# Modulation vectors in four column groups of TensorE, and where their weights are computed

## Chip, core and metric

One NeuronCore of a Trainium2 chip runs the kernel. Its engines work side by side, each on a queue of its own: TensorE (PE; PEld is its weight load), VectorE (DVE), ScalarE (ACT), GpSimd (POOL) and SyncE (SP), which only issues DMAs here. The metric is the device time of one execution in microseconds.

## What is computed

Two layers (`DEPTH = 2`) over 512 latent tokens and 128 context tokens, width `D` = 1024. The part that matters here is the modulation:

```
mod = silu(cvec) @ w_ada + b_ada                  # cvec: c (latent) or c_ctx (context); w_ada is 1024 x 6144
sh1, sc1, g1, sh2, sc2, g2 = split(mod, 6)
u = rmsnorm(h) * (1 + sc1) + sh1                  # feeds q, k, v, the convolution branch and the gates
h = h + g1 * (merged @ w_out)                     # merged: attention and convolution, gated
u2 = rmsnorm(h) * (1 + sc2) + sh2
h = h + g2 * grouped_moe(u2)                      # 16 experts, two for each token
```

`mod` is a pair of rows (latent, context) of 6144 numbers a layer; `w_ada` is 24 MB a layer.

## The kernel before

Weights come in units of 1 MB (`UNIT` = 2048 floats in each of 128 partitions), numbered in the order of use: 8 of `w_ada` (`N_ADA1`), 6 for q, k and v, 4 for the convolution's input, 12 of `w_ada` (`N_ADA2`), 16 for gates and attention output, 4 for the convolution's output, 4 for `w_out`, 4 of `w_ada` (`N_ADA3`), then three for each expert. SyncE loads them in that order. There are two buffers in `raw`; the first `w_ada` units and the experts use two more, `raw_x`. A load waits until the buffer's last user is done (`raw_free`): for a `w_ada` unit that is TensorE, for the others it is the operation that makes `w_lo`. Those other units are split by ScalarE into `w_hi` and by GpSimd into `w_lo = raw - w_hi` (`lo`, L1860 and L1857), for three matmuls in place of one.

A `w_ada` unit goes to TensorE as it is, in fp32. The stationary operand is `cs`, two columns (silu of both vectors), and the weights stream, 512 columns at a time:

```
j, kh = divmod(u, 2)            # unit u: 512 columns of mod (block j), half kh of the 1024 rows
k = kh * 4 + c                  # four matmuls, c = 0..3, sum into the same two rows of one PSUM bank
ins = mm(ps[0:2, b, :], cs[:, :, k], raw_of(ada_unit(u))[:, c * 512:(c + 1) * 512], ...)
```

So two units give one block of 512 columns, and there are 12 blocks. VectorE adds the bias (`mrow`, L1223; `modulation(j)`), for which GpSimd has loaded `adab` (`bias(j)`, two DMAs), and GpSimd stores the block to DRAM (`mod_d`, L1789). At most two blocks are under way, since `mrow` and `adab` have two places.

The start of a layer needs blocks 0 to 3, shift and scale of `u`. When they are in DRAM, GpSimd reads them back as 32 rows of 128 (`mrt`), TensorE turns them (L428), and VectorE makes the columns `mcol`: a copy (L1231), plus 1 on the scale (L1233), times the norm's gain (L1236). ScalarE and VectorE then make `u_hi` and `u_lo` (L909, L1247, L1250), and TensorE starts on q, k and v (L453). GpSimd's queue has the first two `lo` behind the `mrt` loads.

Blocks 4 to 9 lie in the attention. There head h makes its values while the scores of head h + 1 are computed, in an order written out by hand. TensorE has one unit in each of heads 0 to 11, as four pieces of one matmul between `scores`, `p_transposes` and `values`. They all use PSUM bank 7, and a new block waits (`fill`) until VectorE has drained the block before; VectorE does this in heads 2, 4, ... 12. `q_transposes` (L496, L499) stand in odd heads.

Blocks 10 and 11 (half of g2 each) come behind `w_out`: two units ahead of the transposes of `u2`, two around the routing. VectorE drains them behind the routing, and GpSimd stores them ahead of the first gather of the experts.

Of the kernel before, what the change touches and what calls it, by code (L numbers as in the profile page):

```python
# [53 lines left out]
N_ADA1, N_QKV, N_GLU, N_ADA2, N_GATE, N_CO, N_OUT, N_ADA3 = 8, 6, 4, 12, 16, 4, 4, 4  # L54
# [6 lines left out]
U_ADA3 = U_OUT + N_OUT  # L61
U_MOE = U_ADA3 + N_ADA3
# [90 lines left out]
def _build(nc, io, out, ledger, ctx):  # L153
# [116 lines left out]
    gp = const("gp", [P, 2, DH])  # L270
# [17 lines left out]
    adab = at("adab", [2, 2, 512], F32, R_W + 24 * KB)  # L288
    mrow = at("mrow", [2, 2, 512], F32, R_W + 28 * KB)
# [34 lines left out]
    mrt = const("mrt", [32, P])  # L324
# [57 lines left out]
    def _(eng):  # L382
# [19 lines left out]
        with eng.Fori(0, DEPTH) as l:  # L402
# [162 lines left out]
            for h in range(NH):  # L565
# [15 lines left out]
                if modulating:  # L581
                    ada(u, (1,))
# [3 lines left out]
                if modulating:  # L586
                    ada(u, (2,))
# [7 lines left out]
                if modulating:  # L595
                    ada(u, (3,))
# [62 lines left out]

# [1384 lines left out]
```

## Time and profile before

| | us |
|---|---|
| median of 3 runs | 2268.37 |
| lowest, highest run | 2263.72, 2269.03 |
| span of the profiled execution, first to last instruction | 2264.1 |

| engine | busy us | share of the span |
|---|---|---|
| TensorE matmul | 1756.0 | 78% |
| TensorE weight load | 1386.0 | 61% |
| VectorE | 1387.5 | 61% |
| ScalarE | 845.7 | 37% |
| GpSimd | 547.7 | 24% |

The page reports the span of the profiled execution and no time of its own beside it; the runs are other executions. Busy shares are averages over stages with different limits: what an operation is worth is read from its stage, from what the engines there wait for. The mean granted clock of TensorE is 0.885 of full speed. Matmuls overlap in part, so the spacing of two starts says more than the mean duration of one (656 ns in the group of L414).

### The profile page before, as it was taken

To read this page: it belongs to the slowest core of one execution; us is meant where nothing else is said; L and a number is where in the kernel's file an instruction comes from. 1 tells how busy PE (TensorE), PEld (TensorE's weight loads), DVE (VectorE), ACT (ScalarE), POOL (GpSimd) and SP (SyncE) were. 2 spreads that over 40 slices of the span, in tenths; PEclk is the share of its full clock that TensorE was granted. 3 is DMA by queue.
4 is the path that set the end of the run, shared out by engine and by line. 5 is a ranking of instruction groups with operands and counts; after the bars stand their busy time and mean duration, and the time that the engine had idled before them with its cause. 6 is when DMAs were issued, how large, how long until landed. Compare 5 with 4: busy or idle time off the path is not lost.

```text
span 2264.1 us, 29330 instructions
## 1 busy us (share of the span) xinstructions
PE 1756.0 (78%) x8766; PEld 1386.0 (61%) x8766; DVE 1387.5 (61%) x2078; ACT 845.7 (37%) x1294; POOL 547.7 (24%) x388
## 2 busy tenths in 40 slices
PE   5799688888998873888749977888799878658880
PEld 0578454568998751666317874455699876436660
DVE  1458567789854343667462856768898254537754
ACT  2122455571223031657321234556412322147651
POOL 3332000014432223323132220000333222132231
PEclk9799799999999965999979987999899989569995
DMA  8222012112221633989941211211122244359975
GB/s 286 64 59 72 24 57 75 57 38 57 56 75 61 218 130 122 321 305 308 347 156 43 75 43 38 75 57 48 37 76 57 66 163 155 138 184 344 345 245 205
DMA packets 211573, 298.89 MB, mean 132 GB/s; under 512 B 12336, under 2 KB 147696, under 8 KB 211328
## 3 DMA queue, kind: packets, MB, share of 16 engines
q1 hardware_dynamic: 182976, 209.73, 28.6%
q0 software_dynamic: 17872, 46.28, 5.8%
q10 hardware_dynamic: 10560, 40.90, 4.8%
q8 instruction: 76, 1.25, 0.2%
q14 instruction: 89, 0.73, 0.1%
HBM read 267.20 MB, written 39.63 MB: 136 GB/s over the span
## 4 chain that ended last, share of the span: by engine, by line
PE 33%; issue 25%; DVE 18%; DMA 10%; POOL 6%; ACT 5%; DVEq 1%; ACTq 1%; POOLq 0%; SPq 0%
PE ps L467 6%; PE ps L453 5%; PE ps L650 5%; POOL w_lo L1860 5%; PE ps L414 4%; DMA raw<-in_w_down 4%; PE ps L531 2%; PE ps L726 2%; DVE probs L1400 2%; PE ps L511 2%; DVE gu_lo L1206 2%; PE ps L742 2%; PE ps L684 1%; PE ps L513 1%; DMA raw<-in_w_ada 1%
## 5 line engine op out<-in xcount | busy, mean ns | idle before, releaser
L1860 POOL TENSOR_TENSOR w_lo<-raw,w_hi 128x2048 fp32r<-128x2048 f32 (+1 forms) x68 | 298.3, 4393 | 614.9 <-ACT w_hi L887 614.9
L467 PE MATMUL ps<-u_hi,w_hi 128*128 128x320 f32 x768 | 245.9, 320 | 39.5 <-POOL w_lo L1860 29.8
L887 ACT ACTIVATE w_hi<-raw 128x2048 fp32r<-128x2048 f32 (+1 forms) x68 | 109.3, 1610 | 383.5 <-PE ps L453 152.9
L467 PE MATMUL ps<-u_lo,w_hi 128*128 128x320 f32 x768 | 243.5, 317 | 0.0
L467 PE MATMUL ps<-u_hi,w_lo 128*128 128x320 f32 x768 | 243.4, 317 | 0.0
L1510 DVE SCALAR_TENSOR_TENSOR cv<-glu,convw,cv 128x670 f32<-128x670 f32 x240 | 235.2, 1054 | 0.0
L414 PE MATMUL ps<-raw,cs 128*2 128x512 f32 x320 | 173.7, 656 | 30.5 <-DVE mrow L1223 22.3
L467 PEld LDWEIGHTS ps<-u_hi,w_hi 128*128 128x128 f32 x768 | 150.0, 195 | 43.3 <-issue 31.6
L1416 DVE TENSOR_TENSOR pt_lo<-ps,pt_hi 128x512 fp32r<-128x512 f32 x160 | 107.5, 688 | 84.1 <-ACT pt_hi L994 83.4
L994 ACT ACTIVATE pt_hi<-ps 128x512 fp32r<-128x512 f32 x160 | 92.4, 597 | 169.9 <-PE ps L531 168.8
L467 PEld LDWEIGHTS ps<-u_lo,w_hi 128*128 128x128 f32 x768 | 150.2, 196 | 0.1
L467 PEld LDWEIGHTS ps<-u_hi,w_lo 128*128 128x128 f32 x768 | 149.8, 195 | 0.0
L1383 DVE TENSOR_REDUCE nmax<-ps 128x1 f32<-128x640 f32 x128 | 104.3, 815 | 45.1 <-PE ps L513 44.9
L531 PEld LDWEIGHTS ps<-ident,probs 128*128 128x128 f32 x640 | 76.8, 151 | 83.6 <-issue 47.5
L531 PE MATMUL ps<-ident,probs 128*128 128x128 f32 x640 | 104.0, 297 | 24.3 <-DVE probs L1400 19.6
L1789 POOL DMA_DIRECT2D mod_d<-mrow x24 | 12.5, 520 | 451.1 <-DVE mrow L1223 450.2
L453 PE MATMUL ps<-w_hi,u_hi 128*128 128x512 f32 x240 | 97.8, 407 | 29.9 <-DVE u_lo L1250 17.7
L511 PE MATMUL ps<-k_hi,q_st 128*128 128x320 f32 x256 | 90.7, 361 | 38.3 <-DVE q_st L1368 32.5
L971 ACT ACTIVATE probs<-ps,nmax 128x640 f32<-128x640 f32 x128 | 101.3, 792 | 39.5 <-DVE nmax L1383 38.7
L726 PE MATMUL ps<-gu_hi,xt_hi 128*128 128x512 f32 x272 | 107.6, 396 | 5.0 <-DVE xt_lo L1722 5.0
L726 PE MATMUL ps<-gu_hi,xt_lo 128*128 128x512 f32 x272 | 107.1, 394 | 0.0
L726 PE MATMUL ps<-gu_lo,xt_hi 128*128 128x512 f32 x272 | 106.9, 393 | 0.0
(319 smaller groups left out, 4259.5 us busy)
## 6 DMA issues: line engine op xcount, KB each, us to landing
raw<-in_w_ada SPq DMA_DIRECT2D x40, 1024.0 KB
raw<-in_w_in SPq DMA_DIRECT2D x48, 512.0 KB
raw_x<-in_w_gate SPq DMA_DIRECT2D x32, 512.0 KB
raw_x<-in_w_up SPq DMA_DIRECT2D x32, 512.0 KB
raw<-in_w_down SPq DMA_DIRECT2D x16, 1024.0 KB
raw<-in_w_gate SPq DMA_DIRECT2D x32, 512.0 KB
raw<-in_w_up SPq DMA_DIRECT2D x32, 512.0 KB
raw_x<-in_w_down SPq DMA_DIRECT2D x16, 1024.0 KB
```

The costliest lines, as they stand in the source:

```text
L414: ins = mm(ps[0:2, b, :], cs[:, :, k], raw_of(ada_unit(u))[:, c * 512:(c + 1) * 512], start=(k == 0), stop=(k == 7))
L453: ins = mm(ps[:, bs[t], :], (u_hi, u_lo)[x][:, k, t * P:(t + 1) * P], (w_hi, w_lo)[w][:, s, c * 512:(c + 1) * 512], start=(k == 0 and w + ...
L467: ins = mm(ps[:, b, 0:HALF], (w_hi, w_lo)[w][:, s, cols(k):cols(k) + P], xs[x][:, k, half * HALF:(half + 1) * HALF], start=(k == 0 and w + ...
L511: mm(ps[:, b, 0:HALF], q_st[:, h % 2, t * P:(t + 1) * P], k_hi[:, g, i * HALF:(i + 1) * HALF], start=True, stop=False)
L531: ins = nc.tensor.transpose(ps[:, b, t * P:(t + 1) * P], probs[:, h % 2, t, kc * P:(kc + 1) * P], ident[:, :])
L650: ins = mm(ps[:, bs[t], :], (m_hi, m_lo)[x][:, k, t * P:(t + 1) * P], (w_hi, w_lo)[w][:, s, c * 512:(c + 1) * 512], start=(k == 0 and w + ...
L726: ins = mm(ps[:, 2, :], (xt_hi, xt_lo)[x][:, k, :], (gu_hi, gu_lo)[w][i][:, k, :], start=(k == 0 and w + x == 0), stop=(k == 7 and w == 1))
L887: act(w_hi[:, n % 2, 0:k], raw[:, n % 2, 0:k], ACT.Copy).then_inc(*A.up("a_hi", "w_hi", n))
L1383: v.tensor_reduce(nmax[:, h % 2, t:t + 1], ps[:, b0:b0 + 2, 0:HALF], axis=AX.XY, op=ALU.max, negate=True).then_inc(*V.up("v_max", "nmax", ...
L1416: v.tensor_tensor(pt_lo[:, k, :], ps[:, b, :], pt_hi[:, k, :].bitcast(F32), ALU.subtract).then_inc(*V.drained(("PT", h, kc)))
L1510: ins = v.scalar_tensor_tensor(out=cv[:, c, :], in0=src, scalar=convw[:, c, k:k + 1], in1=cv[:, c, :], op0=ALU.mult, op1=ALU.add)
L1860: g_.tensor_tensor(w_lo[:, n % 2, 0:k], raw[:, n % 2, 0:k], w_hi[:, n % 2, 0:k].bitcast(F32), ALU.subtract).then_inc(*G.up("g_lo", "w_lo", n))
```

## The change

A unit of `w_ada` is now one chunk of 128 rows by 2048 columns. Its four matmuls take 512 columns each and write four pairs of PSUM partitions, 0, 32, 64 and 96, which are four column groups of the array. Eight units give one block of 2048 columns, so there are 3 blocks: block 0 is shift and scale of `u` and comes at the start, blocks 1 and 2 come in heads 0 to 7, two units a head. None is left behind `w_out`. `mrow` and `adab` have one place, over 98 partitions, and the bias is added by four VectorE operations of 512 columns, one for each group. Block 0 does not go through DRAM: TensorE turns `mrow` itself, in four transposes of 128 x 128, and four VectorE copies pick the columns.

```diff
-N_ADA1, N_QKV, N_GLU, N_ADA2, N_GATE, N_CO, N_OUT, N_ADA3 = 8, 6, 4, 12, 16, 4, 4, 4
+N_ADA1, N_QKV, N_GLU, N_ADA2, N_GATE, N_CO, N_OUT = 8, 6, 4, 16, 16, 4, 4
@@ TensorE
-            def ada(u, rows, bank=None):
-
-                j, kh = divmod(u, 2)
-                b = fill(("ada", j), bank) if kh == 0 and rows[0] == 0 else fills.of["ada", j]
...
+            def ada(u, bank=None):
+
+                j, k = divmod(u, KC)
+                b = fill(("ada", j), bank) if k == 0 else fills.of["ada", j]
+                eng.wait_ge(*T.at("w_raw", ada_unit(u)))
+                for q in range(4):
+                    ins = mm(ps[32 * q:32 * q + 2, b, :], cs[:, :, k], raw_of(ada_unit(u))[:, q * 512:(q + 1) * 512], start=(k == 0), stop=(k == KC - 1))
...
-            eng.wait_ge(*T.at("mrt"))
-            eng.sem_inc(sems("passed_T"), 1)
-            ins = nc.tensor.transpose(ps[:, b, 0:32], mrt[:, :], ident[0:32, 0:32])
+            eng.wait_ge(*T.at("drained", ("ada", 0)))
+            for c in range(4):
+                ins = nc.tensor.transpose(ps[:, b, c * P:(c + 1) * P], mrow[:, c * P:(c + 1) * P], ident[:, :])
@@ TensorE, head h
-                    ada(u, (0,), 7)
+                    ada(N_ADA1 + 2 * h, 7)
                 scores(h + 1, 0)
...
                 scores(h + 1, 1)
-                if modulating:
-                    ada(u, (1,))
...
                 scores(h + 1, 2)
                 if modulating:
-                    ada(u, (2,))
+                    ada(N_ADA1 + 2 * h + 1, 7)
...
                 values(h, 4)
-                if modulating:
-                    ada(u, (3,))
@@ TensorE, behind w_out
-            for u in range(N_ADA1 + N_ADA2, N_ADA1 + N_ADA2 + 2):
-                ada(u, range(4), 7)
@@ SyncE
-                load(n, (r(n, 4), io["w_ada"][l, kh * 512:(kh + 1) * 512, j * 512:(j + 1) * 512].rearrange("(c p) n -> p c n", p=P)))
+                load(n, (raw_of(n), io["w_ada"][l, k * P:(k + 1) * P, j * UNIT:(j + 1) * UNIT]))
@@ VectorE
-                v.tensor_tensor(mrow[:, j % 2, :], ps[0:2, b, :], adab[:, j % 2, :], ALU.add).then_inc(*V.drained(("ada", j)))
+                for q in range(4):
+                    rows = slice(32 * q, 32 * q + 2)
+                    ins = v.tensor_tensor(mrow[rows, :], ps[rows, b, :], adab[rows, :], ALU.add)
...
-            v.tensor_copy(mcol[:, :, :, :].rearrange("p a b c -> p (a b c)"), ps[:, b, 0:32]).then_inc(*V.drained(("mcol",)))
+            for i in range(2):
+                for a in range(2):
+                    ins = v.tensor_copy(mcol[:, i, a, :].rearrange("p (y c) -> p y c", y=2), turned[:, a, :, :, i])
...
-                if h % 2 == 0 and 2 <= h <= 12:
-                    modulation(3 + h // 2)
+                if h in (4, 8):
+                    modulation(h // 4)
@@ GpSimd
-            for j in range(4):
-                modulation(j)
-                if j + 2 < 4:
-                    bias(j + 2)
...
-            for i in range(2):
-                dma(mrt[i * 16:(i + 1) * 16, :], mod_d[i, 0:2 * D].rearrange("(r p) -> r p", p=P), "mrt", *(("mrt",) if i else ()))
...
-            modulation(10)
-            modulation(11)
```

On TensorE's queue, the first part of a head before (`raw` is the modulation's first matmul of the head; rows with `k_hi`, `probs` and `v_hl` are scores, transposes and values):

```order
L414 MATMUL ps<-raw,cs 2x512
L508 REGISTER_ALU
L390 REGISTER_ALU
L511 MATMUL ps<-k_hi,q_st 128x320
L513 MATMUL ps<-k_lo,q_st 128x320
L511 MATMUL ps<-k_hi,q_st 128x320
L513 MATMUL ps<-k_lo,q_st 128x320
L531 MATMUL ps<-ident,probs 128x128 x4
L390 REGISTER_ALU
L540 MATMUL ps<-pt_hi,v_hl 128x512
L540 MATMUL ps<-pt_lo,v_hl 128x512
```

and the end of one of heads 0 to 7 of the change, around its second unit:

```order
L504 MATMUL ps<-k_hi,q_st 128x320
L506 MATMUL ps<-k_lo,q_st 128x320
L406 REGISTER_ALU
L408 MATMUL ps<-raw,cs 2x512 x4
L386 REGISTER_ALU
L524 MATMUL ps<-ident,probs 128x128 x4
L533 MATMUL ps<-pt_hi,v_hl 128x512
L533 MATMUL ps<-pt_lo,v_hl 128x512
```

A single matmul at four places of a head has become a row of four at two places.

On GpSimd's queue, the start of a layer before (`ISA` and `REGISTER_ALU` rows are waits):

```order
L1834 ISA
L1789 DMA mod_d<-mrow 2x512
L1834 ISA
L1789 DMA mod_d<-mrow 2x512
L1848 ISA
L1789 DMA mrt<-mod_d 16x128 x2
L1855 ISA
L1860 TENSOR_TENSOR w_lo<-raw,w_hi 128x2048
L1855 REGISTER_ALU
L1860 TENSOR_TENSOR w_lo<-raw,w_hi 128x2048
```

and of the change, at the same place:

```order
L1772 DMA adab<-in_b_ada 2x512
L1772 ISA
L1772 DMA n1col<-in_n_cols 128x8
L1827 ISA
L1830 ISA
L1835 TENSOR_TENSOR w_lo<-raw,w_hi 128x2048
L1830 REGISTER_ALU
L1835 TENSOR_TENSOR w_lo<-raw,w_hi 128x2048
```

The stores and the `mrt` loads are gone, and the first `w_lo` stands behind one wait, for the bias adds of block 0 (L1827), and that for its `w_hi` (L1830).

## Rows read from the trace of the kernel before

**Rows 1.** The page's costliest groups: the line of the modulation matmuls.
```profile
L414 PE MATMUL ps<-raw,cs 128*2 128x512 f32 x320 | 173.7, 656 | 30.5 <-DVE mrow L1223 22.3
```

**Rows 2.** The chain that ended last (start, length, what), both layers' starts.
```profile
31.21 17.34 PE ps L414 x40
...
54.92 1.74 DMA mrt<-mod_d
57.43 7.02 DVE mcol L1233
...
1114.51 22.02 DMA y_in<-y_d
...
1146.36 3.18 DMA adab<-in_b_ada
1152.12 3.66 DMA adab<-in_b_ada
...
1162.38 6.95 DVE mcol L1233
```

**Rows 3.** Timeline, first layer's start: start us, us, engine, line, operation, [idle before].
```profile
9.78 9.68 PE L414 MATMUL ps<-raw_x,cs 128*2 128x512 f32 x16 [9.78 <-POOL mrt L1815]
...
34.64 7.03 PE L414 MATMUL ps<-raw_x,cs 128*2 128x512 f32 x16
...
48.58 0.68 DVE L1223 TENSOR_TENSOR mrow<-ps,adab 2x512 f32<-2x512 f32 x1 [5.98 <-PE ps L414]
...
50.45 1.91 ACT L887 ACTIVATE w_hi<-raw 128x2048 fp32r<-128x2048 f32 x1 [25.21 <-DMA raw<-in_w_in]
...
55.42 8.97 POOL L1860 TENSOR_TENSOR w_lo<-raw,w_hi 128x2048 fp32r<-128x2048 f32 x2
...
57.21 0.19 DVE L1231 COPY mcol<-ps 128x32 f32<-128x32 f32 x1 [7.95 <-PE ps L428]
```

**Rows 4.** Busy time by stretch: length, PE, PEld, DVE, ACT, POOL, PEclk, DMA, GB/s.
```profile
31.20:41.00 9.80, 9.79 (x23) 1.96 (x24) 0.68 (x1) 0.00 (x0) 3.03 (x6) 1.00 1.03 383
41.00:48.60 7.60, 7.54 (x18) 1.36 (x16) 0.70 (x2) 0.00 (x0) 0.51 (x1) 1.00 0.30 88
```

**Rows 5.** The same view, second layer's start.
```profile
1130.00:1137.70 7.70, 3.13 (x8) 0.48 (x6) 4.82 (x4) 2.07 (x4) 1.07 (x2) 1.00 1.04 413
```

**Rows 6.** Timeline, second layer's start, POOL.
```profile
1160.30 8.98 POOL L1860 TENSOR_TENSOR w_lo<-raw,w_hi 128x2048 fp32r<-128x2048 f32 x2
```

**Rows 7.** Timeline behind the output projection of layer one.
```profile
811.13 10.82 POOL L1857 TENSOR_TENSOR gu_lo<-raw_x,gu_hi 128x2048 fp32r<-128x2048 f32 x2 [7.13 <-ACT gu_hi L891]
812.07 5.54 DVE L1565 SCALAR_TENSOR_TENSOR u<-h_a,rstd,a_row 128x1024 f32<-128x1024 f32 x1
```

**Rows 8.** Busy time by stretch: heads 1 to 7, heads 8 to 11, single heads.
```profile
276.25:387.22 110.97, 94.21 (x436) 56.08 (x435) 80.35 (x167) 59.71 (x142) 4.53 (x9) 0.94 0.21 67
387.22:451.98 64.76, 54.67 (x249) 32.35 (x248) 45.56 (x95) 33.60 (x80) 2.01 (x4) 0.92 0.22 66
339.74:354.30 14.56, 12.92 (x67) 7.66 (x66) 11.96 (x26) 9.32 (x22) 0.00 (x0) 1.00 0.24 74
354.30:372.64 18.34, 14.93 (x61) 8.75 (x61) 10.86 (x23) 7.48 (x18) 1.49 (x3) 0.81 0.19 59
1559.72:1571.51 11.79, 9.57 (x55) 6.70 (x55) 10.85 (x23) 7.65 (x18) 0.51 (x1) 1.00 0.16 46
1571.51:1584.25 12.74, 9.15 (x58) 7.31 (x58) 12.07 (x26) 9.38 (x22) 0.00 (x0) 1.00 0.00 1
```

**Rows 9.** Timeline of PE in heads 5 and 6.
```profile
348.29 1.02 PE L414 MATMUL ps<-raw,cs 128*2 128x512 f32 x2
...
357.15 1.09 PE L531 MATMUL ps<-ident,probs 128*128 128x128 f32 x8 [0.68 <-DVE probs L1400]
...
360.64 1.87 PE L414 MATMUL ps<-raw,cs 128*2 128x512 f32 x2 [2.23 <-DVE mrow L1223]
```

**Rows 10.** Timeline ahead of the experts, POOL.
```profile
886.91 1.13 POOL L1789 DMA_DIRECT2D mod_d<-mrow  x2 [0.19 <-issue]
```

More of the change, by code:

```diff
@@ L1824, in bias @@
             def bias(j):
[L1826 to L1827 removed]
+                if j >= 1:
+                    eng.wait_ge(*G.at("drained", ("ada", j - 1)))
                     eng.sem_inc(sems("passed_G"), 1)
[L1829 to L1830 removed]
+                for q in range(4):
+                    dma(adab[32 * q:32 * q + 2, :], io["b_ada"][bass.ds(l, 1), j * UNIT + q * 512:j * UNIT + (q + 1) * 512].broadcast_to([2, 512]),
+                        "ada_b", *(("ada_bias", j) if q == 3 else ()))
             def modulation(j):
@@ L1835, in modulation @@
                 eng.sem_inc(sems("passed_G"), 1)
-                dma(mod_d[:, j * 512:(j + 1) * 512], mrow[:, j % 2, :], f"mod_st{j % 2}", "mod_out", j)
+                for q in range(4):
+                    dma(mod_d[:, j * UNIT + q * 512:j * UNIT + (q + 1) * 512], mrow[32 * q:32 * q + 2, :], "mod_st", *(("mod_out", j) if q == 3 else ()))
             bias(0)
-            bias(1)
             dma(n1col[:, :], io["n1_cols"][l], "g_n1", "n1_loaded")
-            for j in range(4):
-                modulation(j)
-                if j + 2 < 4:
-                    bias(j + 2)
-            eng.wait_ge(*G.at("mod_out", 2))
+            eng.wait_ge(*G.at("drained", ("ada", 0)))
             eng.sem_inc(sems("passed_G"), 1)
-            eng.wait_ge(*G.at("mod_out", 3))
-            eng.sem_inc(sems("passed_G"), 1)
-            for i in range(2):
-                dma(mrt[i * 16:(i + 1) * 16, :], mod_d[i, 0:2 * D].rearrange("(r p) -> r p", p=P), "mrt", *(("mrt",) if i else ()))
             def lo(n):
@@ L1889, in _ @@
             eng.sem_inc(sems("passed_G"), 1)
-            bias(4)
-            bias(5)
+            bias(1)
             eng.wait_ge(*G.at("k_done", LT))
@@ L1898, in _ @@
             g_.memset(ssq[:, 6:7], 0.0).then_inc(*G.up("g_c", "kv_free"))
-            for j in range(4, 10):
-                modulation(j)
-                if j + 2 < 10:
-                    bias(j + 2)
-            eng.wait_ge(*G.at("mod_out", 8))
-            eng.wait_ge(*G.at("mod_out", 9))
-            for n in range(U_GATE, U_ADA3):
+            modulation(1)
+            bias(2)
+            modulation(2)
+            eng.wait_ge(*G.at("mod_out", 2))
+            for n in range(U_GATE, U_MOE):
                 lo(n)
-            eng.wait_ge(*G.at(*used(U_ADA3 - 1)))
-            eng.sem_inc(sems("passed_G"), 1)
-            bias(10)
-            bias(11)
             for n in range(U_MOE, U_MOE + 2):
```

71 lines of the change are left out of this document (28 added, 43 removed).

## Prediction

> **What bounds the kernel now.** I read the chain that ended last first, to see which stages hold the end; then the timeline of each stage that the change touches; then the busy time by stretch for clock, DMA and the period of a head.
>
> Three places matter. First, the start of each layer. The reader is to see one line that is never parallel: TensorE computes units 3 to 7 back to back for 17.34 us, 40 records at 0.43 us each [rows 2]. VectorE then adds the bias (0.68 us), the row goes to DRAM and comes back by DMA, and TensorE turns it. VectorE's small `mcol` operation then takes 7.02 us (6.95 in the second layer) instead of a fraction of one, and it ends where GpSimd's two `w_lo` operations end (55.42 + 8.97 = 64.39; 57.43 + 7.02 = 64.45) [rows 2, 3]. The same pair ends at 1169.28 in the second layer and releases the same operation [rows 2, 6]. In the second layer the chain before it is not TensorE's but the bias DMAs: 3.18 us, then 3.66 us, one bank pair after the other [rows 2].
>
> Second, the attention heads. An odd head with its four modulation pieces takes 14.56 us with TensorE busy for 12.92 of it; a head without them takes 11.79 (even) or 12.74 us (odd), and VectorE is then the busiest (10.85 and 12.07) [rows 8]. So TensorE is the bound in heads 1 to 11 and VectorE in heads 12 to 15. Even heads take up to 18.34 us [rows 8]: TensorE stands 2.23 us until VectorE has drained bank 7, and comes out at the low clock (two records in 1.87 instead of 1.02 us) [rows 9].
>
> Third, ahead of the experts, two `mod_d` stores stand on GpSimd's queue before the first gather, 1.13 us [rows 10].
>
> **The price on which all hangs: a unit's four matmuls.** Before, one unit is four matmuls, each of which leaves two records in the trace (320 records for the 40 units in `raw` [rows 1]; 16 records, two units, in 7.03 us [rows 3]), so a unit takes 3.43 us at 2.4 GHz and twice that at 1.2. All write column group 0. After, the four write groups 0 to 3. No row here shows two matmuls in different groups. Bounds: nothing overlaps, 8 x 0.43 = 3.43 us; everything overlaps, two records deep, 0.86 us. Between them: a matmul's own two records go to the same group, so the second waits for the first, and if the queue also starts its instructions in program order, only the second record of one matmul lies beside the first of the next: 5 steps of 0.43 = 2.14 us for a unit alone. I take this value, because the 0.43 us spacing of all 40 records [rows 2] shows same-group records strictly behind each other; this is argued, not seen.
>
> The Trainium skill (TensorE: Matmul & The Clock Gate, Part 3: Packing small matmuls) gives 2.38x for three column tiles; carried on to four that would be an estimate of about 1.1 us for a unit, near the lower bound, and the sum would be some 2205 us. The same section says that a weight load overlaps a running matmul only where the row group differs; here all four share the rows, which would put a unit near the upper bound. No run here shows either.
>
> **Heads.** A piece (two records) holds TensorE for about 1.0 us [rows 9]; a lump of one unit would hold it 2.14 + 0.1 = 2.25. Each of heads 0 to 7 loses four pieces and gets two lumps, at the places of the first and third. First and third: +1.25 each. Second: -1.0. The fourth was free already, since TensorE waits 0.68 us for `probs` behind it [rows 9]. Sum +1.5; VectorE is near its own pace, so I take +1.3. Over heads 1 to 7 that is +9.1. Of their three stalls on bank 7 two go: the even head of the rows is 3.8 us longer than the odd one [rows 8], 3.5 taken, so -7.0. The one left (head 4) has four VectorE operations of 0.68 ahead instead of one: +2.0. So 110.97 becomes 115.1. Head 0: +1.3. Heads 8 to 11 lose everything: 64.76 us becomes twice 11.79 + 12.74 = 49.1, plus 2.7 for the modulation's four operations at head 8, which are now on the bounding engine: 51.8, a gain of 13.0 [rows 8]. Net 13.0 - 4.1 - 1.3 = 7.6 a layer, **15 us in both**. What is late next is VectorE. Its extra time at head 8 also holds the maxima queued behind it.
>
> **First layer's start.** TensorE stops being the bound and the loads take over: DMA is full until 41 us (share 1.03 at 383 GB/s) and nearly idle after it (0.30) [rows 4]. The eight units are the same 8 MB, so the last lands near 41 however fast TensorE is; its unit ends near 43 instead of 48.6. Then four bias adds (2.7), four transposes (8 take 1.09 [rows 9], so 0.5 to 0.8), four copies of at most 0.19 [rows 3]: `mcol`'s scalar operation is asked for near 47.3. Removed: a store, a load and the waits between (54.92 and before [rows 2]). But GpSimd's first `w_lo` now waits for the bias adds alone, and its `w_hi` began at 50.45 [rows 3], 5.3 us after TensorE released unit 6 (48.55 - 3.43 = 45.1), and took 1.91. With the release near 40.5 it ends near 47.3 to 47.7. The pair then holds VectorE until about 56.4 instead of 64.4: **8 us** (3 if TensorE stays the bound; 17 if `mcol` gets in first and what it meets afterwards is hidden). If it gets in first, `w_lo` meets the u pipeline instead, where one VectorE operation took 5.54 us beside GpSimd [rows 7], so most of the 9 us of the pair are paid again.
>
> The Trainium skill (SBUF — State Buffer, SBUF: two separate sides) says that the shared port is held for one whole instruction by whoever starts first. Row 57.43 shows VectorE waiting for both GpSimd instructions, so the measurement decides; by the rule alone VectorE would get in after the first, 4.5 us earlier a layer.
>
> **Second layer's start.** One group of four bias DMAs replaces the chain of pairs; its last lands where the second pair's did, 1149.5 [rows 2]. Bias adds to 1152.3, `w_lo` starts at 1152.6 instead of 1160.30: 7.7 us, and `mcol` waits for the pair again. Against it: DMA is saturated there (1.04, 413 GB/s [rows 5]) while `y_in` is on the chain for 22.02 us [rows 2]. Units 4 to 7 are now asked for earlier and in rows of 8 KB instead of 2 KB, so they take more of it. Up to 2.1 MB (two units) more ahead of `y_in` is 5 us; I take 2.5. **5 us.**
>
> **Ahead of the experts.** Two stores and their waits go, 1.3 us a layer: **2.6 us**. The four late units' matmuls cost nothing before: they lay beside VectorE's routing. The earlier loads of expert weights are hidden too.
>
> **Sum.** 15 + 8 + 5 + 2.6 = 30.6. The profiled execution's span is 2264.1, so 2233.5; the median of the runs is 4.3 above that span, so **2238 us**. A measurement of this kernel tells about 0.3%, 7 us, from no change.
>
> **Rivals.** *Full overlap* (0.86 us): lumps cost what a piece did, each head of 0 to 7 gets 1.0 shorter, heads give 52 us, the first start 11 (the last unit ends 1.3 us earlier, and in one case in four `mcol` gets in first): 70.6 in all, **2198 us**. For it: the groups share no output. Against: each matmul's two records. *No overlap* (3.43 us), the one on the other side: a lump is 3.54, each of eight heads grows by 2 x 2.54 - 1.0 = 4.1 (16 units where 12 were). Heads lose 29 us, the first start gives 3, the second 6, the experts 2.6: **2286 us**. Between 2.14 and 3.43 us a unit the sum goes from +30.6 to -17.4; it decides from about 2.96 us a unit, where the sum is nil. For it: every record in rows 1 to 3 is spaced as if alone. *The clock falls in heads 8 to 15*, where nothing fills TensorE any more: against it, heads without pieces ran at clock 1.00 with TensorE busy 9.57 of 11.79 us [rows 8]. If it did, a head grows by 0 to 7.4 us (twice 9.57 less 11.79), say 3.5, times 16: **2294 us**; it outweighs the gain from 1.9 us a head.
>
> **How the numbers follow.** Half overlap 0.47, full 0.20, none 0.20, clock 0.05, another mixture 0.08 (mostly faster). Faster 0.74, within 0.3% 0.06, slower 0.20. The range for eight in ten reaches from below full overlap, 2190, almost to none, 2285; half overlap alone gives 2224 to 2252, from the bounds of the first start and of the slip.
>
> **What would show it.** In the new trace: first to last start of a unit's eight records at 2.4 GHz: 1.7 to 2.1 us (half), under 1 (full), 3.4 (none). Heads 1, 3 near 15.9 us; heads 9, 10 near 12. `w_lo`'s first pair at about 47.5 and 1152.6 to 1155, with `mcol` ending beside it. `y_in` landing up to 3 us later than 1136.5. I am wrong if units overlap otherwise, if `w_lo` is later for want of `w_hi`, or if the lumps starve VectorE in heads 0 to 7.

## The result, and the profile after

| | us |
|---|---|
| before, median of 4 runs beside it | 2266.88 (2263.72 to 2269.03) |
| after, median of 4 runs | 2207.85 (2198.12 to 2209.05) |
| ratio, 95% interval | 0.9737 [0.9714, 0.9760] |
| span of the profiled execution after | 2196.6 |

The change is faster by 59 us, where the forecast had 30: the direction held, and the time lies inside the range, but at the place of a rival, full overlap (2198 us), not of the case that was called likeliest. The profiled execution (2198.12 us) is some 10 us below the other three, which have no trace; heads 8 to 12 below show one place that differs by 6 us from layer to layer.

The group that was most expensive for the modulation [rows 1], in the list of groups of the changed kernel (busy us, mean ns of one, idle before):

```profile
L408 PE MATMUL ps<-raw,cs 128*2 128x512 f32 x320 | 50.1, 706 | 22.4 <-DMA raw<-in_w_ada 17.3 <-DVE mrow L1201 5.0
```

The same 320 records keep TensorE busy for 50.1 us instead of 173.7, although one lasts a little longer. The next view, busy time in two short windows of one unit in head 1 at 2.4 GHz (length, PE, PEld, clock), shows why:

```profile
268.40:268.80 0.40, 0.36 (x4) 0.11 (x8) 1.00 0.00 0
268.40:269.50 1.10, 1.04 (x8) 0.11 (x8) 1.00 0.00 0
```

Four of the eight records run within the first 0.4 us, and all eight are done after 1.04 us: two rounds of four side by side, one round 0.43 us behind the other, and the last record is shown as 0.59 us long. The eight weight loads are all in the first window. The forecast took 2.14 us for this.

The chain that ended last, both layers' starts [rows 2]:

```profile
14.61 26.50 DMA adab<-in_b_ada
...
45.69 3.35 DVE mcol L1219
...
1073.22 28.49 DMA y_in<-y_d
...
1111.69 1.85 DMA adab<-in_b_ada
...
1118.13 3.10 DVE mcol L1219
```

TensorE is gone from the first start; what ends last is a DMA, the bias, which stands on GpSimd's queue behind the copies of `x_all` to `h_d`. The timeline of the first start [rows 3]:

```profile
38.92 1.89 PE L408 MATMUL ps<-raw,cs 128*2 128x512 f32 x8 [6.43 <-DMA raw<-in_w_ada]
41.13 2.84 DVE L1201 TENSOR_TENSOR mrow<-ps,adab 2x512 f32<-2x512 f32 x4 [4.76 <-DMA adab<-in_b_ada]
44.02 1.11 PE L421 MATMUL ps<-ident,mrow 128*128 128x128 f32 x4 [3.22 <-DVE mrow L1201]
44.47 8.98 POOL L1835 TENSOR_TENSOR w_lo<-raw,w_hi 128x2048 fp32r<-128x2048 f32 x2 [28.77 <-ACT w_hi L864]
45.69 3.34 DVE L1219 TENSOR_SCALAR mcol<-mcol 128x16 f32<-128x16 f32 x1
49.06 4.49 DVE L1222 TENSOR_TENSOR mcol<-mcol,n1col 128x8 f32<-128x8 f32 x2
```

TensorE stands 6.43 us for the last unit and is done 1.9 us after it starts. VectorE's first `mcol` operation ends with GpSimd's first `w_lo` (45.69 + 3.34 = 49.03; a `w_lo` takes half of 8.98), the next two with the second, at 53.5. "The pair" below means these two `w_lo`.

The heads, busy time by stretch [rows 8]: heads 1 to 7 and 8 to 11 of the first layer, then of the second:

```profile
263.54:361.88 98.34, 78.95 (x491) 53.23 (x491) 81.52 (x168) 60.25 (x142) 4.00 (x8) 0.95 0.45 151
361.88:413.61 51.73, 36.42 (x217) 29.42 (x216) 47.48 (x97) 34.18 (x80) 1.99 (x4) 0.97 0.03 7
...
1336.67:1435.88 99.21, 80.38 (x491) 54.62 (x491) 81.51 (x168) 60.30 (x142) 4.04 (x8) 0.93 0.45 149
1435.88:1490.95 55.07, 41.25 (x216) 35.01 (x216) 48.33 (x97) 34.10 (x80) 1.99 (x4) 0.85 0.02 7
```

110.97 us have become 98.34, and 64.76 have become 51.73 and 55.07. The account of both profiled executions, from the starts of the first or last record at each mark (q, k, v; the context's transpose in a head; the convolution's branch; the transposes of `xe`, the rows gathered for the experts):

| stretch | layer 1, before, after | layer 2, before, after |
|---|---|---|
| start of the layer to q, k, v (layer 2: from the last `xe`) | 83.6, 72.8 | 88.9, 85.6 |
| to head 0 | 192.6, 190.7 | 195.8, 191.7 |
| head 0 to head 12 | 187.5, 161.3 | 187.2, 167.4 |
| to the branch | 35.3, 36.8 | 37.5, 39.6 |
| to the first `xe` | 395.7, 394.6 | 394.7, 393.9 |
| experts | 204.8, 203.1 | 203.2, 203.0 |
| end, behind the last `xe` | | 57.2, 55.9 |

The stretches join, so the gains sum to the 67.5 us by which the spans differ: 46 in the heads, 14 in the starts, 2 ahead of the experts. The second row's 6 us were not forecast and lie, up to head 0, where the change touches nothing. In the first layer the convolution's input took 21.87 us at clock 1.00 after and 24.27 at 0.89 before. In the second, q, k, v and what follows them, before and after:

```profile
1188.50:1283.17 94.67, 88.57 (x361) 72.26 (x361) 40.42 (x45) 14.80 (x16) 25.07 (x8) 0.92 0.20 59
```
```profile
1144.93:1234.98 90.05, 83.95 (x361) 68.73 (x361) 38.97 (x41) 14.80 (x16) 25.44 (x8) 0.98 0.21 62
```

So these 6 us go, as far as they are traced, with a clock that came out otherwise in this execution, and the change itself is worth some 61 us of the 67.5; the medians say 59.

### The profile page after: what moved, and what is told of

Same layout as the page of the kernel before. It is cut to its first block, busy times and chain, and to the rows that moved or that the text cites. A ratio compares the mean times of both kernels' runs of the same rounds, so it can differ in the third digit from the quotient of the medians.

```text
span 2196.6 us, 29390 instructions
## 1 busy us (share of the span) xinstructions
PE 1626.6 (74%) x8772; PEld 1377.6 (63%) x8772; DVE 1393.7 (63%) x2084; ACT 847.4 (39%) x1294; POOL 530.5 (24%) x352
## 4 chain that ended last, share of the span: by engine, by line
PE 35%; issue 26%; DVE 17%; DMA 9%; POOL 6%; ACT 4%; DVEq 1%; ACTq 0%; POOLq 0%
PE ps L460 10%; PE ps L638 5%; PE ps L446 5%; POOL w_lo L1835 4%; DMA raw<-in_w_down 3%; PE ps L707 3%; PE ps L524 2%; PE ps L723 2%; DVE gu_lo L1182 2%; DMA y_in<-y_d 2%; PE ps L667 1%; DMA raw_x<-in_w_down 1%; PE ps L408 1%; DMA adab<-in_b_ada 1%; PE ps L504 1%
## 5 line engine op out<-in xcount | busy, mean ns | idle before, releaser
L524 PEld LDWEIGHTS ps<-ident,probs 128*128 128x128 f32 x640 | 84.0, 157 | 66.8 <-DVE probs L1386 33.4
L1705 DVE TENSOR_TENSOR xt_lo<-ps,xt_hi 128x1024 fp32r<-128x1024 f32 x36 | 44.1, 1225 | 104.0 <-ACT xt_hi L1117 104.0
L691 PE MATMUL ps<-ident,xe 128*128 128x128 f32 x288 | 42.2, 295 | 73.8 <-DMA xe<-u_d,gidx 73.8
```

The source lines that it names most:

```text
L524: ins = nc.tensor.transpose(ps[:, b, t * P:(t + 1) * P], probs[:, h % 2, t, kc * P:(kc + 1) * P], ident[:, :])
```

## The experiments

Each time stands beside its ratio to the kernel before on the same chip. Where an edit changes values, the router sends other numbers of rows to the experts, and that stage is then longer or shorter for a reason of its own: the count of `xe` transposes, from the lists of groups of the changed kernel and of rows_2k:

```profile
L691 PE MATMUL ps<-ident,xe 128*128 128x128 f32 x288 | 42.2, 295 | 73.8 <-DMA xe<-u_d,gidx 73.8
```
```profile
L691 PE MATMUL ps<-ident,xe 128*128 128x128 f32 x312 | 44.1, 288 | 75.1 <-DMA xe<-u_d,gidx 75.1
```

Of the first four runs I therefore compare stages, not times. Marks as in the account above; "start 2" is from the last `xe`; heads are 0 to 8 and 8 to 12, both layers. Each row is one execution. In spread and the kernels built on it (both_starts, adds_first, first_place), heads 8 to 12 also hold units and the second drain of bank 7, which the changed kernel has ahead of them:

| kernel | start 1 | start 2 | heads 0 to 8 | heads 8 to 12 |
|---|---|---|---|---|
| before | 83.6 | 88.9 | 128.1, 129.3 | 59.4, 57.9 |
| changed | 72.8 | 85.6 | 113.4, 113.3 | 47.9, 54.2 |
| one_group | 73.5 | 83.7 | 140.3, 144.2 | 48.1, 50.0 |
| two_abab | 72.8 | 84.0 | 121.8, 123.9 | 48.0, 48.0 |
| two_aabb | 72.9 | 84.6 | 124.4, 121.8 | 48.0, 51.5 |
| rows_2k | 75.4 | 84.2 | 113.2, 113.2 | 49.1, 54.2 |
| through_dram | 78.1 | 90.9 | 113.2, 113.1 | 54.2, 54.2 |
| lo_behind | 72.9 | 84.8 | 113.3, 114.4 | 49.1, 54.2 |
| stores_later | 68.3 | 80.2 | 113.2, 113.2 | 49.1, 49.1 |
| y_first | 73.2 | 80.3 | 113.1, 114.3 | 49.3, 52.8 |
| spread | 72.5 | 85.1 | 113.9, 112.6 | 57.3, 57.4 |
| both_starts | 67.9 | 76.7 | 112.7, 110.5 | 57.3, 57.3 |
| adds_first | 70.0 | 76.1 | 112.5, 112.6 | 57.3, 57.4 |
| filler | 72.8 | 84.7 | 113.2, 114.4 | 49.8, 49.9 |
| first_place | 67.9 | 73.5 | 106.4, 106.4 | 53.5, 53.5 |

### The unit's price: one_group, two_abab, two_aabb

```diff
                 for q in range(4):
-                    ins = mm(ps[32 * q:32 * q + 2, b, :], cs[:, :, k], ...
+                    g = q if k in (0, KC - 1) else 0        # two_abab: q % 2, two_aabb: q // 2
+                    ins = mm(ps[32 * g:32 * g + 2, b, :], cs[:, :, k], ...
```

> Units 1 to 6 of each block of eight put all four matmuls into column group 0 (units 0 and 7 stay as they are), so three quarters of the modulation is left out of the result; instructions, operands and waits are the same. Theory (the unit's price is the term that was mis-sized: the four groups run fully side by side): such a unit takes 8 x 0.43 = 3.43 us instead of 1.04 at 2.4 GHz, heads 1 to 7 grow by about 2 x 2.4 us each where both units are affected, 12 units a layer by 2.4 = 29 us, 57 in both layers, so about 2265 us. Rival (the gain came from fewer pieces and fewer stalls on bank 7, and the lump's length lies beside VectorE's work): less than half of that, 2220 to 2235 us.

> Units 1 to 6 of each block use two column groups in the order 0, 1, 0, 1 (half of the modulation is left out of the result). If every group is served by itself, each has two matmuls of two records, 4 x 0.43 = 1.72 us a unit instead of 1.04: +0.7 us for 24 units, about 2225 us. Strictly in program order it is the same 1.72, since neighbours always differ. If two groups only half overlap, as the prediction took for four: 8 records in 6 steps, 2.6 us, 2245 us.

> As two_abab, but in the order 0, 0, 1, 1 (half of the modulation is left out of the result). Theory that a matmul whose group is busy blocks those behind it, so that order counts: group 1 starts only when the last record of group 0 has started, 1.29 + 1.72 = 3.0 us a unit, +2.0 us for 24 units, about 2255 us. Rival that each group has a queue of its own and order doesn't matter: 1.72 us, as two_abab, about 2225 us.

Measured: 2244.87 us (ratio 0.9908 [0.9876, 0.9939]), 2198.62 (0.9708 [0.9674, 0.9742]) and 2217.52 (0.9805 [0.9767, 0.9842]), all with fewer rows in the experts (272, 272 and 280 transposes, where the changed kernel has 288; the experts of one_group take 196.6 and 193.4 us instead of 203, 16 of the 20 us by which 2265 was missed). One unit in a head of each, in the order above, by the timeline:

```profile
276.12 3.60 PE L409 MATMUL ps<-raw,cs 128*2 128x512 f32 x8
```
```profile
273.18 1.89 PE L409 MATMUL ps<-raw,cs 128*2 128x512 f32 x8
```
```profile
270.15 1.89 PE L409 MATMUL ps<-raw,cs 128*2 128x512 f32 x8
```

3.60, 1.89 and 1.89 us stand against 1.04 with four groups (seven, three, three and one steps of 0.43 us from the first start to the last, and 0.59 for the last record). Two_aabb is the one that tells most. The same windows as above show how many records run in its first 0.4 us, and in all, with one_group's first 0.4 us below:

```profile
270.10:270.50 0.40, 0.35 (x2) 0.10 (x4) 1.00 0.00 0
270.10:272.10 2.00, 1.89 (x8) 0.30 (x8) 1.00 0.00 0
```
```profile
276.10:276.50 0.40, 0.39 (x1) 0.09 (x2) 1.00 0.00 0
```

Two records run at once from the start in two_aabb, and in one_group only one. Records of one group start 0.43 us apart there, so the second record is group 1's, although in the program its first matmul stands behind all four records of group 0. So each group is served by itself, and a busy group doesn't hold the matmuls behind it: order within four matmuls cost nothing. The theory that a busy group blocks the others falls.

In the heads, one_group has 27 and 31 us more between heads 0 and 8, 2.4 to 2.8 for each of the 11 affected units there: the lumps lie on the path at their full price. The rival (their length is hidden beside VectorE) falls too. The two-group kernels have 8 to 11 us more.

### What the change does for the starts: through_dram, rows_2k, lo_behind

through_dram undoes one part, the turning of `mrow` by TensorE:

```diff
-            eng.wait_ge(*G.at("drained", ("ada", 0)))
+            modulation(0)
+            eng.wait_ge(*G.at("mod_out", 0))
             eng.sem_inc(sems("passed_G"), 1)
+            for i in range(2):
+                dma(mrt[i * 16:(i + 1) * 16, :], mod_d[i, 0:2 * D].rearrange("(r p) -> r p", p=P), "mrt", ...)
```

> The changed kernel with one part undone: block 0 goes from mrow to DRAM (four stores), comes back as 32 rows of 128 (mrt) and is turned by one transpose, and GpSimd's first two w_lo stand behind these DMAs, as before the change. Theory (the part is worth what GpSimd's pair is put back by): the bias adds end at 44.0, the store and its wait take about 5.6 us as before the change, so the pair starts near 49.6 instead of 44.5, mcol waits for it, and q, k, v start 5 us later in each layer: about 10 us more than the changed kernel, 2218 us. Rival (mcol gets in ahead of or between the pair, so that only the row's own way counts): 1 to 3 us a layer, 2210 to 2214 us.

2224.46 us, 0.9811 [0.9785, 0.9837]. Both starts are 5.3 us longer, as the theory said. In its timeline the pair begins at 49.91 and `mcol` ends with it:

```profile
48.87 1.03 POOL L1767 DMA_DIRECT2D mrt<-mod_d  x2 [2.19 <-DMA mod_d<-mrow]
49.91 9.00 POOL L1833 TENSOR_TENSOR w_lo<-raw,w_hi 128x2048 fp32r<-128x2048 f32 x2
51.68 0.19 DVE L1212 COPY mcol<-ps 128x32 f32<-128x32 f32 x1 [7.61 <-PE ps L422]
51.91 7.04 DVE L1214 TENSOR_SCALAR mcol<-mcol 128x16 f32<-128x16 f32 x1
```

The median is 16.6 us above the changed kernel's, the profiled span 26.2 us (2222.8 and 2196.6). Of the 26.2, 10.6 are these, 6.3 are heads 8 to 12 of the first layer (54.2 where the changed kernel's profile has 47.9), 3.9 the experts, and most of the rest lies ahead of head 0 and behind head 12: stages that the edit doesn't touch. What the 6 us in the medians beyond these 10.6 are isn't shown, as the other executions have no trace.

rows_2k loads the units as before the change:

```diff
-                load(n, (raw_of(n), io["w_ada"][l, k * P:(k + 1) * P, j * UNIT:(j + 1) * UNIT]))
+                load(n, (r(n, 4), io["w_ada"][l, kh * 512:(kh + 1) * 512, j * 512:(j + 1) * 512].rearrange("(c p) n -> p c n", p=P)))
```

> The w_ada units are loaded as before the change, 512 columns of 512 rows, in rows of 2 KB instead of 8 KB, and multiplied as if they were the others (same bytes, the modulation's values are wrong). Theory (8 KB rows take more of the DMA engines while y_in, in 4 KB rows, waits beside them): y_in takes some 22 to 24 us again instead of 28.5, and the time falls by up to 5 us, to about 2203 us. Rival (y_in is late because units 4 to 7 are asked for sooner, now that TensorE is through them faster, whatever their rows): 27 to 29 us, no change of the time beyond 2 us.

2237.68 us, 0.9886 [0.9848, 0.9923], with 24 transposes more in the experts, which took 211.9 and 224.8 us instead of 203; so the expected times can't be read from it. By stage: the last `y_in` tile comes 22.9 us after the last issue (1090.16 to 1113.03) where the changed kernel's chain has 28.49, so the size of the rows bears on how the DMA engines are shared. (In the kernels that load rows of 8 KB and leave the issue of loads and stores as it is, the last tile lands 26.2 to 28.5 us after its issue.) The last unit lands later for it in the first layer (TensorE is through it at 44.3 instead of 40.8). Start 1 is 2.6 us longer. Start 2, 84.2, lies among the 83.7 to 85.6 of the kernels with rows of 8 KB and a start otherwise unchanged: the rows of 8 KB cost nothing in sum.

lo_behind moves the pair behind `mcol`:

```diff
-            eng.wait_ge(*G.at("drained", ("ada", 0)))
+            eng.wait_ge(*G.at("acol"))
             eng.sem_inc(sems("passed_G"), 1)
             def lo(n):
```

> The changed kernel, but GpSimd waits for the finished mcol (acol) before its first two w_lo, not for the bias adds alone. Theory (paid again): mcol is done near 46.8 instead of 53.6 and u starts 6.8 us earlier, but the pair, now beside VectorE's u pipeline, costs about what it held VectorE for; in the run with rows of 2 KB one w_lo beside it lengthened the pipeline by 4.1 us, so two cost 8 us: between 2 us faster and 2 us slower a layer, 2204 to 2212 us. Rival (the pair fits into VectorE's waits for ScalarE in the pipeline): 5 to 6.8 us a layer less, about 2196 us.

2208.81 us, 0.9740 [0.9713, 0.9768], no change, and starts of 72.9 and 84.8. Without the pair beside it the last steps of `mcol` take 0.4 us instead of 7.9:

```profile
46.62 0.17 DVE L1219 TENSOR_SCALAR mcol<-mcol 128x16 f32<-128x16 f32 x1
46.82 0.24 DVE L1222 TENSOR_TENSOR mcol<-mcol,n1col 128x8 f32<-128x8 f32 x2
```

`u_hi` starts at 49.06 instead of 53.67, and `u_lo` is nevertheless done at 72.35, where it was 72.21: the gain goes back into the `u` pipeline beside the pair. "Paid again" holds.

### Emptying the DMA queues at the starts: stores_later, y_first

```diff
-        for t in range(NT):
-            dma(h_d[t * P:(t + 1) * P, :], io["x_all"][t * P:(t + 1) * P, :], "h_st")
...
             dma(lnb[:, :], io["ln_b_cols"][l], "g_small", "small_loaded")
+            for t in range(NT):
+                eng.wait_ge(*G.at("h", t, previous=True))
+                eng.sem_inc(sems("passed_G"), 1)
+                dma(h_d[t * P:(t + 1) * P, :], h_cur[:, t, :], "h_st", "h_stored", t)
```

> The copy of x_all to h_d (2.6 MB from DRAM to DRAM, ahead of the first layer) and the stores of h_cur at the end of each layer become five stores of h_cur behind the first two w_lo of each layer. Theory (in the first layer the loads are the bound, and this copy shares the DMA engines with them until 41 us): the last w_ada unit lands near 32 to 34 us instead of 38.9, q, k, v start 5 us earlier in the first layer; in the second, the bias lands earlier, but VectorE comes to the adds only 1 us earlier, since xn ends at 1112.3 and the adds began at 1113.6: together 6 us less, about 2202 us. Rival (the copy takes a share that the loads couldn't use): no change of the first start beyond 1 us, 2207 us.

2197.41 us, 0.9694 [0.9661, 0.9728]. Start 1 falls by 4.5 us. TensorE is through the last unit at 35.4 (33.50 + 1.89), and the adds no longer wait for the bias; VectorE comes to them from `xn`:

```profile
33.50 1.89 PE L408 MATMUL ps<-raw,cs 128*2 128x512 f32 x8 [0.93 <-DMA raw<-in_w_ada]
36.39 2.83 DVE L1201 TENSOR_TENSOR mrow<-ps,adab 2x512 f32<-2x512 f32 x4
```

Start 2 fell by 5.4 us, of which I had expected 1: the stores shared the DMA engines with `y_in` too (from the last `xe` to the last tile 38.7 us instead of 42.4). That is 3.7 of the 5.4; the rest isn't traced.

```diff
+                    if n == 4:
+                        eng.wait_ge(*S.at("y_here", previous=True))    # VectorE raises it behind its wait for the fourth tile
                     eng.wait_ge(*S.at(*raw_free(n - 4)))
```

> The changed kernel, but SyncE issues units 4 to 7 of the second layer only when the fourth of the five y_in tiles has landed. Theory (y_in is late because these 4 MB share the DMA engines with it): y_in is landed 10 to 12 us after its first issue instead of 31, VectorE then sets the pace with 3.8 us a tile, h_cur is done near 1096 instead of 1105.5, and q, k, v start 8 to 9 us earlier in the second layer, about 2199 us. Rival (all bytes are needed anyway, and the w_in units for the first w_lo then come late by as much): no gain, 2205 to 2210 us.

2197.53 us, 0.9686 [0.9663, 0.9709]. VectorE now goes through `y_in` without a wait, and the last tile is taken up 31.5 us after the last `xe` instead of 42.4. 5.6 of these 10.9 us are lost again: units 4 to 7 were released only at 1094, and TensorE ends the last at 1113.65. Start 2 is 80.3, in between the two theories; `y_in` is landed 18.7 us after its first issue, not 10 to 12.

### The heads and the clock: spread, both_starts, adds_first, filler, first_place

```diff
-                modulating = 2 * h < N_ADA2
-                if modulating:
-                    ada(N_ADA1 + 2 * h, 7)
+                if h < 4:
+                    ada(N_ADA1 + 2 * h, 7)
...
-                if modulating:
-                    ada(N_ADA1 + 2 * h + 1, 7)
+                if h < 12:
+                    ada(N_ADA1 + 2 * h + 1 if h < 4 else N_ADA1 + 4 + h, 7)
```

Block 2 is drained in head 12 instead of head 8.

> The changed kernel, but the 16 units lie two in each of heads 0 to 3 and one, at the second place, in each of heads 4 to 11. Theory (a lone unit fits into TensorE's waits for VectorE): in the changed kernel a pair of heads with two units each takes 26.1 us and one without 24.0 at the high clock, so heads 4 to 11 would take 4 x 24.0 = 96 us, where four heads with two units and four without take 2 x 26.1 + 3.7 for the stall of head 4 + 48 = 104: 4 to 8 us less a layer. And if heads 8 to 13 lose the clock because TensorE is idle in them, they keep it: 7 us less in each layer that had lost it. Together about 2190 us. Rival (a unit costs its 0.5 us wherever it lies): nothing from the first part, and 2200 to 2208 us, depending on the clock alone.

2214.17 us, 0.9776 [0.9748, 0.9805]: no gain, and both theories miss it, since an odd head with one unit takes longer (15.04 us) than one with two (13.74). Its clock by stretch, heads 9 and 10 of the second layer, and what TensorE did in the first of them:

```profile
1463.79:1478.83 15.04, 11.57 (x66) 8.93 (x66) 12.14 (x26) 9.22 (x22) 0.00 (x0) 0.89 0.20 70
1478.83:1491.08 12.25, 9.60 (x61) 6.75 (x61) 10.19 (x22) 7.54 (x18) 0.00 (x0) 1.00 0.22 85
```
```profile
1465.71 0.66 PE L489 MATMUL ps<-ident,q_tok 128*128 128x128 f32 x4 [0.69 <-ACT ctxp L960]
1467.33 0.33 PE L492 MATMUL ps<-ident,q_tok 128*128 128x128 f32 x1 [0.96 <-DVE cpt_lo L1407]
1467.52 1.06 PE L524 MATMUL ps<-ident,probs 128*128 128x128 f32 x8
1468.34 0.31 PE L550 MATMUL ps<-cpt_hi,v_hl 128*128 128x128 f32 x1
1468.48 0.27 PE L550 MATMUL ps<-cpt_lo,v_hl 128*128 128x128 f32 x1
1470.07 0.63 PE L504 MATMUL ps<-k_hi,q_st 128*128 128x320 f32 x1 [1.32 <-DVE q_st L1353]
1470.50 0.47 PE L506 MATMUL ps<-k_lo,q_st 128*128 128x320 f32 x1
```

TensorE idles 0.69, 0.96 and 1.32 us, with matmuls between, and what follows the last runs at 1.2 GHz (0.47 us for the second `scores` matmul, which takes 0.31 at the high level). In the changed kernel a unit lies in that last gap in heads 0 to 7, and nothing does in heads 8 to 15. Filler puts matmuls there that nobody reads:

```diff
+                if 9 <= h < NH - 1:
+                    if h == 9:
+                        eng.wait_ge(*T.at("drained", ("ada", 2)))
+                    for q in range(4):
+                        mm(ps[32 * q:32 * q + 2, 7, :], cs[:, :, 0], mrow[:, :], start=True, stop=True)
```

> The changed kernel, with four more matmuls that nobody reads (four column groups, 512 columns, as a unit) at the first place of each of heads 9 to 14, the result is unchanged. Theory (the clock falls in heads 8 to 13 because TensorE idles there, 1.07 and 1.31 us ahead of q_transposes' last and of scores in an odd head, 1.50 us ahead of p_transposes in an even one, and in a layer where it has fallen it doesn't come back): with the gaps ahead of scores filled, heads 9 to 13 show 1.00, a pair takes 24.0 to 24.6 us in both layers, and the layer that took 54.2 us for heads 8 to 11 takes 48 to 50: about 2203 us. Rival (the gap ahead of p_transposes or of ctx scores decides, and the dummies only add work): 50 to 57 us in both, 2208 to 2218 us.

2196.57 us, 0.9694 [0.9673, 0.9714], where the changed kernel has 0.9737: the two intervals just touch, so more work cost nothing and may have gained. Heads 8 to 12 take 49.8 and 49.9 us. That alone settles nothing: changed, rows_2k, through_dram, lo_behind, stores_later and y_first have the same heads without filler, and their twelve layers take from 47.9 to 54.2 us, six of them under 49.8. Head by head it says more. Head 9 shows a clock of 0.88 or less in eleven of these twelve layers, and 1.00 in both of filler, as heads 11 and 13 do there. An even head still falls to 0.87 (10 in the first layer, 12 in the second). Heads 9 and 10 of the second layer, in the changed kernel and in filler:

```profile
1449.94:1463.83 13.89, 10.24 (x58) 8.65 (x58) 12.29 (x26) 9.32 (x22) 0.00 (x0) 0.88 0.01 1
1463.83:1476.89 13.06, 10.72 (x53) 9.49 (x53) 10.56 (x22) 7.71 (x18) 0.00 (x0) 0.74 0.00 1
```
```profile
1455.83:1468.58 12.75, 10.16 (x67) 7.43 (x66) 12.02 (x26) 9.41 (x22) 0.00 (x0) 1.00 0.00 1
1468.58:1479.94 11.36, 9.17 (x61) 6.97 (x61) 10.40 (x22) 7.69 (x18) 0.00 (x0) 1.00 0.00 1
```

Two kernels put the edits together, both_starts:

> Three edits together: h_d stored behind the first two w_lo (as in stores_later), units 4 to 7 of the second layer issued when the fourth y_in tile has landed (as in y_first, but released by ScalarE at its landing, not by VectorE behind its work), and the units spread over heads 0 to 11 (as in spread). If the effects add: first start 68.3 us instead of 72.8; in the second layer y_first gave the loads away for 5.6 us because VectorE released them late, so experts' end to q, k, v falls from 85.6 to 74 to 76 us; heads as in spread. About 2185 us. If the two edits on the second start share one effect (both only empty the DMA engines beside y_in), it stays at 80 us, 2190 us.

and adds_first:

> both_starts, and VectorE adds the bias of block 0 before it makes xn, not after. If the adds and the turning can lie beside the wait for std in the second layer, q, k, v start there up to 3 us earlier than in both_starts. Rival: GpSimd's pair starts earlier too and holds xn as it held mcol: no gain, or up to 5 us more.

2192.03 us, 0.9680 [0.9657, 0.9704] and 2196.37, 0.9698 [0.9673, 0.9722]. Start 2 of both_starts is 76.7, so the two edits add nearly (8.9 us, where they gave 5.4 and 5.3 alone); the heads are as slow as in spread. first_place below has the same edits there and shows 73.5, so this mark of one execution is good to some 3 us. In adds_first VectorE's five `xn` took from 37.77 to 49.67 us in the first layer, across the pair, instead of 3.4: the first start is 2.1 longer; the second is 0.6 shorter, which is within what one execution tells.

first_place is both_starts with the lone unit at the head's first place:

```diff
-                if h < 4:
-                    ada(N_ADA1 + 2 * h, 7)
+                if h < 4 or 4 < h < 12:
+                    ada(N_ADA1 + 2 * h if h < 4 else N_ADA1 + 4 + h, 7)
```

> both_starts, with the lone unit of heads 5 to 11 at the first place of the head (ahead of scores) in place of the second. In spread and both_starts an odd head with a lone unit took 15.04 us at clock 0.89, one with two 13.75 at 1.00. Theory (what counts is the gap ahead of scores, which a unit at the first place fills): odd heads 12.9 to 13.75, even ones 11.3 to 12.3, at 1.00, so a pair takes 24.2 to 26.1 us instead of 27.3, 4 to 11 us less a layer: 2170 to 2185 us. Rival (the place doesn't matter, a lone unit keeps TensorE busy too little): 15.0 and 12.3 again, 2192 us.

**2171.29 us, 0.9598 [0.9577, 0.9619]**, the fastest of all, 1.4% of the time before below the changed kernel's ratio. In heads 5 to 11 of each layer the lone unit now lies ahead of `scores` (head 4's stays at the second place). The next view is the busy time of heads 7 to 10 of the second layer:

```profile
1402.65:1415.38 12.73, 10.16 (x66) 7.40 (x66) 11.98 (x26) 9.44 (x22) 0.00 (x0) 1.00 0.25 83
1415.38:1426.76 11.38, 9.11 (x61) 6.90 (x61) 10.40 (x22) 7.70 (x18) 0.00 (x0) 1.00 0.28 94
1426.76:1439.56 12.80, 10.15 (x66) 7.43 (x66) 11.98 (x26) 9.44 (x22) 0.00 (x0) 1.00 0.24 84
1439.56:1452.55 12.99, 10.81 (x61) 7.72 (x61) 10.49 (x22) 7.81 (x18) 0.00 (x0) 0.87 0.29 81
```

Heads 7 to 9 run at 1.00, and with one unit each they take within 0.14 us what heads with none take at that clock (12.73 and 11.24 in the changed kernel's first layer); head 10 still falls to 0.87, and I have no cause for it. The kernel to compare with is both_starts, which differs in nothing but the place: heads 0 to 12 take 159.9 us in both layers instead of 170.0 and 167.8, 18 of the 20.7 us between the medians. The odd heads 5 to 11 are at 1.00 in both layers; in spread, both_starts and adds_first 23 of 24 such heads are at 0.89. The one that isn't, head 5 of both_starts' second layer, tells the clock from the rest:

```profile
1398.10:1411.85 13.75, 10.37 (x66) 7.46 (x66) 11.92 (x26) 9.32 (x22) 0.00 (x0) 1.00 0.23 78
```

At the second place a unit makes an odd head 1.0 us longer at the full clock (13.75 instead of 12.73), and the low clock adds 1.3 (15.04). In the even heads, at 1.00 in both kernels, the place alone is worth 0.9 us (12.25 and 11.38). The place decides, not the number.

## Why the prediction was right and wrong

**The unit's price is the step that failed.** It was put as "if the queue also starts its instructions in program order, only the second record of one matmul lies beside the first of the next: 5 steps of 0.43 = 2.14 us". A unit took 1.04 us at 2.4 GHz, which by the spacing of starts is two rounds of 0.43, the 0.86 us of the rival that the forecast gave a chance of 0.20. The first half of the argument holds (a group's own records are 0.43 us apart), the second doesn't: two_aabb shows that a group's matmuls start while those ahead of them wait. The reason given for the value, the even spacing of all records before, could not tell: all of them were in one group. The Trainium skill (TensorE: Matmul & The Clock Gate, Part 3: Packing small matmuls) was the better guide with its 2.38x for three column tiles: two groups gave 3.60 / 1.89 = 1.9, four 3.60 / 1.04 = 3.5. Its sentence that a weight load overlaps a running matmul only where the row group differs isn't borne out here, where all four share the rows: the eight weight loads lie within the first 0.4 us, beside four running records.

**Heads 1 to 7**: forecast 110.97 to 115.1 us, measured 98.34 and 99.21 (the latter from 112.14). The lump was put at 2.25 us, and 14 of them cost 1.2 each too much: 16.8 us, the whole difference in the first layer (one_group confirms the price, not that the forecast's other terms were each right). Heads 1 and 3 took 13.74 and 13.90, not 15.9. That lumps lie on the path was right, by one_group. So was the stall of head 4, 17.66 us.

**Heads 8 to 11**: forecast 51.8, measured 51.73 in the first layer. That this agrees to 0.1 us is in part luck. Head 8 took 15.03 us at clock 0.89 where the forecast's terms give 14.5 (11.79 + 2.7), and head 10 took 11.24 where 11.79 was. The row of 11.79 us [rows 8] had been read as a head without pieces, but it still holds the last piece of head 11:

```profile
1560.88 1.02 PE L414 MATMUL ps<-raw,cs 128*2 128x512 f32 x2
```

In the second it was 55.07, and there the rival "the clock falls in heads 8 to 15" came true in part: 0.74 to 0.88 in heads 9 to 14, and heads 9 to 13 each 1.2 to 1.9 us longer than in the first layer, about half of the 3.5 it was priced at. The argument against it, that heads without pieces ran at 1.00 before, rested on two of them [rows 8], and one had this piece in it. With matmuls in the stretch ahead of `scores`, the odd heads kept 1.00 in filler and in first_place, so that stretch is a cause in odd heads. The even heads, and why heads with the same stretches kept the clock in the first layer, stay open.

**First start**: forecast 8, measured 10.8. The unit ended at 40.8 instead of 43, since the last load landed at 38.9 and the unit took 1.9 us at the low clock. The pair, at 44.5 instead of 47.5, held `mcol` to its end, as forecast, though in two steps: the first operation got in after the first `w_lo`, as the Trainium skill (SBUF — State Buffer, SBUF: two separate sides) has it, while in through_dram the same operation waited 7.04 us for both. Nothing came of it, since the next two operations waited for the second `w_lo`. Not foreseen: the bias landed 0.3 us behind the last unit.

**Second start**: forecast 5, measured 3.2. The slip of `y_in` was put at 2.5 us. Its piece of the chain grew by 6.5 (22.02 to 28.49), and the last tile was taken up 42.4 us after the last `xe` where it had been 36.9, 5.5 us later; rows_2k, with 22.9 us, shows the row size as the main reason. From there to q, k, v it is 43.2 us where it was 51.9: 8.7 rather than 7.7.

**Ahead of the experts**: forecast 2.6, measured 1.1 and 0.8.

Put together: 15 was 42 us in the heads (46 less 3.6 lost behind head 12), 8 was 10.8, 5 was 3.2, 2.6 was 1.9. With 1.2 us less for each of the 16 lumps of a layer and nothing else changed, the prediction's own sum gives 30.6 + 2 x 19.4 = 69 us. The profiled executions differ by some 61 without the clock ahead of head 0. The 8 us between are for the most part the clock too: 3.3 us in heads 8 to 11 of the second layer, and of the 3.6 behind head 12 at least head 13 of the second layer, 14.10 us at 0.88 where it had taken 12.74 at 1.00.

## What to carry to other kernels

Matmuls with few stationary columns that go to different column groups ran side by side here in both orders that were tried, fp32 too: price them by the fullest group, not by their count. Before a wait of TensorE is called free, look whether the matmuls behind it run at the high clock: here a unit in a gap of 1.3 us cost an odd head 0.1 us, and the same unit some matmuls later 2.3 us, 1.0 for itself and 1.3 for the clock. Where a start waits for loads, count what else the DMA engines carry then: 2.6 MB of copies that nobody needed yet cost 4.5 us.

## What the runs showed of the hardware

- Two fp32 matmuls in different column groups overlap even if both of the busy group's matmuls stand ahead in the queue: records 13 ns apart in two_aabb, 0.429 us apart within a group. Four groups: eight records in 1.04 us (the changed kernel), one group: 3.60 (one_group).
- Idle stretches of 0.69, 0.96 and 1.32 us in a head were followed by 1.2 GHz (spread); with matmuls in the third, which cut it to 0.34 us, the head stayed at 1.00 (filler, first_place).
- A VectorE operation of 0.17 us (lo_behind) took 3.34 beside GpSimd's pair and got in between its two operations (the changed kernel); in through_dram the same one waited for both (7.04 us).
- Rows of 8 KB took DMA time from rows of 4 KB beside them: 28.5 (the changed kernel) instead of 22.9 us (rows_2k) for the last tile of `y_in`.
